# One transformer kernel, one core: the expert sum of the PEER layer, half as a dense pass and half as a gather

## The chip, the core and the metric

The kernel runs on one core of one Trainium2 chip, as one launch. The metric is the device time of that core in microseconds (us), the median of several runs. The core has five engines that run beside each other, each through its own list of instructions: TensorE (PE in the profile; PEld is its weight load), VectorE (DVE), ScalarE (ACT), GpSimd (POOL) and SyncE (SP). They wait for each other on semaphores. DMA transfers are started by SP (queue q1) and by POOL (queue q0, for transfers whose addresses are in a table in SBUF).

## What is computed

The reference runs two blocks on 256 tokens of width 2048, all in float32. The first block ends with a PEER layer (product-key experts); the second block begins with a norm of its result. Only the PEER layer and the norms behind it are touched. Cut to what matters:

```python
# per token: 8 heads, in each the 16 best of 128 x 128 experts (pairs of two key numbers)
# expert number = 128 * key0 + key1, 16384 experts; 8 * 16 = 128 picks per token
w    = softmax(scores of the 16 best)
dot  = sum(h * peer_down[expert])            # down row: 2048 floats, 8 KB
x    = x + gt2 * sum_picks(w * gelu(dot) * peer_up[expert])   # up row: 8 KB
x    = rmsnorm(x, final_g)                   # end of block 1
h    = rmsnorm(x, g_pre) ; proj = h @ w_in   # start of block 2
```

The 256 tokens are two blocks of 128 (`tb` 0 and 1), one token on each of the 128 partitions. "Pick" p (0 to 255) is the p-th pick of all 128 tokens of a block: picks 0 to 127 belong to block 0, 128 to 255 to block 1. One gather fetches one pick: 128 rows, one per partition.

## The kernel before

The program is five phases, with a barrier of all engines between them: modulation, projection and first block up to about 971 us, `phase_peer` (the touched one), then the second projection and the second merge. In the second part PE runs without a gap over weights that ACT and POOL split in two.

**phase_peer** starts with a short prelude: ACT and PE turn the keys and the normed tokens `h2`, PE makes the first queries and scores, DVE makes the lists of route 0. A "route" is one head of one block of tokens (16 routes); its lists give 16 picks. Then comes one loop over `G` = 0 to 127, two picks per G, written out on each engine:

- **POOL** (`block.gpsimd`, L1662 and L1670) issues per G two gathers of `peer_down` rows into `down_rows` and two of `peer_up` rows into `up_rows`, 1 MB each. Both tiles have 4 slots (`ROWS`), so a gather waits until the pick four before it has been used.
- **DVE** makes the two dot products of the G (L2057, 128x2048 each), then a part of the lists of a coming route at some G (`key_list` twice, `pair_list`, `pick_numbers`, `normalize`, at `lists_at(r)`: every 8 G up to route 7, then every 6 G, up to G = 104), then adds the up row of the even pick, times its share, to `expert_sum` (`add_even`, L2017, 128x2048).
- **ACT** makes gelu and share of the two picks and a diagonal matrix of the odd pick's share (`pick_diagonal`).
- **PE** adds the odd pick's up row by four matmuls of the diagonal with 512 columns each (L1764) into four PSUM banks. Between these it works through the remaining queries, the scores, and from `G = KV` on the key/value projection of `mem` for block 2 (L1792), whose weights SP loads through `weight_ring`.

At `G = TAIL` = 64 the sum of block 0 is complete; its residual, its norms and its turned copy are made inside the loop. After the loop the same is done for block 1 in four column pieces of 512, and the first weight tile of `w_in_2` is split.

An fp32 matmul stands in the trace as two records.

## Time and profile before

| | us |
|---|---|
| median of 3 runs (3496.9 to 3499.43) | 3499.34 |
| span of the profiled execution | 3498.0 |
| from its start to the first dot product of the loop | 1002.75 |
| end of the last dot product of the loop | about 2323.4 |
| first matmul of the second projection | 2349.80 |

The profiled execution is 1.3 us under the median of the runs. The page gives one line for each costly group of instructions, with its busy time, the mean of one, and the idle time just ahead of it on its engine with what ended that idle time. The timeline view gives start and length of single instructions. A duration can overlap the next one's start by some tens of ns, so where many of the same kind follow each other, the distance from start to start is the cost.

### The profile page before, as it was taken

The numbers are of one execution on the slowest core, as the hardware profiler recorded it, in microseconds if no ns is written. First come the engines' busy times: TensorE is split into PE (matmuls) and PEld (weight loads), VectorE is DVE, ScalarE is ACT, GpSimd is POOL, SyncE is SP. The second block draws the span as 40 slices with busy tenths as digits, with TensorE's granted clock in tenths as the row PEclk, the third lists the DMA queues.
The fourth block names the chain that finished last, engine by engine and source line by source line (L and its number), as shares of the span: only waits on it lengthen the run. The fifth ranks groups of instructions, "written<-read, shape, count | busy, mean of one in ns | idle before, by whom it ended". The sixth has DMA issues, their size and how long they took to land. (4 is left out here: it accounts for less than half of the span.)

```text
span 3498.0 us, 31036 instructions
## 1 busy us (share of the span) xinstructions
PE 2928.4 (84%) x11330; PEld 2066.9 (59%) x11330; DVE 1862.3 (53%) x2379; ACT 1143.5 (33%) x1853; POOL 2390.3 (68%) x1133
## 2 busy tenths in 40 slices
PE   5899999999976666665456776569999999999999
PEld 1687778788853333322122232238888888888887
DVE  0767365532457787868888787761137421111121
ACT  2422354454421111111122112124445344444443
POOL 0444675688836676757677666758767688888887
PEclk9999999999988888877777887779999999999999
DMA  9899753455669999999999999986545455666554
GB/s 414 296 346 347 248 165 127 133 193 187 234 263 427 425 427 425 427 425 428 415 427 427 425 427 404 427 336 202 172 155 191 133 181 193 212 204 204 191 188 169
DMA packets 305995, 1015.86 MB, mean 290 GB/s; under 512 B 21916, under 2 KB 26616, under 8 KB 234928
## 3 DMA queue, kind: packets, MB, share of 16 engines
q1 hardware_dynamic: 228870, 472.46, 39.1%
q0 software_dynamic: 73728, 536.90, 36.4%
q10 hardware_dynamic: 3244, 4.51, 0.3%
q8 instruction: 90, 1.47, 0.2%
q14 instruction: 63, 0.51, 0.0%
HBM read 1009.58 MB, written 4.23 MB: 290 GB/s over the span
## 5 line engine op out<-in xcount | busy, mean ns | idle before, releaser
L670 POOL TENSOR_TENSOR block_weights_lo<-weight_ring,block_weights_hi 128x1024 fp32r<-128x1024 f32 x608 | 1483.6, 2449 | 611.1 <-ACT block_weights_hi L663 498.6
L1764 PE MATMUL banks<-up_rows,pick_diagonal 128*128 128x512 f32 x1024 | 675.4, 821 | 469.4 <-DMA up_rows<-peer_up,picked_experts 403.1
L663 ACT ACTIVATE block_weights_hi<-weight_ring 128x1024 fp32r<-128x1024 f32 x608 | 641.2, 1059 | 976.0 <-PE banks L2831 315.8
L1764 PEld LDWEIGHTS banks<-up_rows,pick_diagonal 128*128 128x128 f32 x1024 | 261.8, 268 | 852.2 <-issue 745.6
L1670 POOL DMA_INDIRECT up_rows<-peer_up,picked_experts x256 | 477.4, 1865 | 338.2 <-PE banks L1764 113.4
L2057 DVE CUSTOM_DVE_ANT_0 down_rows<-down_rows,h_tokens 128x2048 f32<-128x2048 f32 x256 | 584.3, 2290 | 203.2 <-DMA down_rows<-peer_down,picked_experts 198.3
L1662 POOL DMA_INDIRECT down_rows<-peer_down,picked_experts x256 | 422.3, 1649 | 116.2 <-issue 79.5
L2017 DVE SCALAR_TENSOR_TENSOR expert_sum<-up_rows,pick_share,expert_sum 128x2048 f32<-128x2048 f32 x125 | 293.9, 2351 | 57.9 <-ACT pick_share L1887 52.7
L1881 ACT ACTIVATE pick_gelu<-pick_dots 128x2 f32<-128x2 f32 x127 | 25.8, 203 | 828.1 <-DVE pick_dots L2057 828.0
L2264 PE MATMUL banks<-block_weights_hi,h_T_hi 128*128 128x512 f32 x704 | 282.2, 401 | 2.7 <-PEq L1534 2.7
L2266 PE MATMUL banks<-block_weights_hi,h_T_lo 128*128 128x512 f32 x704 | 275.2, 391 | 0.0
L2265 PE MATMUL banks<-block_weights_lo,h_T_hi 128*128 128x512 f32 x704 | 274.8, 390 | 0.0
L2829 PE MATMUL banks<-block_weights_hi,h_T_hi 128*128 128x512 f32 x640 | 250.2, 391 | 0.0
L2831 PE MATMUL banks<-block_weights_hi,h_T_lo 128*128 128x512 f32 x640 | 249.3, 390 | 0.0
L2830 PE MATMUL banks<-block_weights_lo,h_T_hi 128*128 128x512 f32 x640 | 249.1, 389 | 0.0
L940 PE MATMUL banks<-block_weights_hi,h_T_hi 128*128 128x512 f32 x512 | 205.2, 401 | 6.8 <-POOL block_weights_lo L670 5.2
L589 DVE SCALAR_TENSOR_TENSOR banks<-cond_ring,cond_T,banks 128x512 f32<-128x512 f32 x224 | 169.3, 756 | 64.4 <-DMA cond_ring<-w_ada 57.6
L941 PE MATMUL banks<-block_weights_lo,h_T_hi 128*128 128x512 f32 x512 | 200.7, 392 | 0.0
L2895 DVE TENSOR_TENSOR gate<-banks,p_cols 128x512 f32<-128x512 f32 x32 | 20.6, 686 | 262.4 <-PE banks L2831 262.4
L2264 PEld LDWEIGHTS banks<-block_weights_hi,h_T_hi 128*128 128x128 f32 x704 | 132.6, 188 | 31.4 <-issue 4.8
L942 PE MATMUL banks<-block_weights_hi,h_T_lo 128*128 128x512 f32 x384 | 150.5, 392 | 0.0
L2266 PEld LDWEIGHTS banks<-block_weights_hi,h_T_lo 128*128 128x128 f32 x704 | 132.5, 188 | 28.3
(500 smaller groups left out, 4412.2 us busy)
## 6 DMA issues: line engine op xcount, KB each, us to landing
weight_ring<-w_in SPq DMA_DIRECT2D x232, 1024.0 KB, 5.0
cond_ring<-w_ada SPq DMA_DIRECT2D x128, 512.0 KB, 6.1
weight_ring<-w_ada SPq DMA_DIRECT2D x32, 1024.0 KB, 8.6
weight_ring<-w_out SPq DMA_DIRECT2D x32, 1024.0 KB, 5.0
weight_ring<-peer_query SPq DMA_DIRECT2D x16, 1024.0 KB, 16.3
weight_ring<-w_ret_out SPq DMA_DIRECT2D x8, 1024.0 KB, 4.9
weight_ring<-w_mlstm_out SPq DMA_DIRECT2D x8, 1024.0 KB, 4.9
weight_ring<-w_mem_kv SPq DMA_DIRECT2D x8, 1024.0 KB, 16.4
```

Of the source, the lines that this page charges most:

```text
L663: act.activation(self.hi[:, self.place(slot, h)], ring.tile[:, slot, h * self.HALF:(h + 1) * self.HALF], ACT.Copy).then_inc(self.hi_ready, 1)
L670: pool.tensor_tensor(self.lo[:, at], ring.tile[:, slot, h * self.HALF:(h + 1) * self.HALF], self.hi[:, at], ALU.subtract).then_inc(ring.us ...
L1662: pool.indirect_dma_start(down[:, p % ROWS], None, io["peer_down"][0], bass.IndirectOffsetOnAxis(ap=expert[:, p:p + 1], axis=0)).then_inc( ...
L1670: pool.indirect_dma_start(up[:, p % ROWS], None, io["peer_up"][0], bass.IndirectOffsetOnAxis(ap=expert[:, p:p + 1], axis=0)).then_inc(up_l ...
L1764: mm = pe.matmul(ps[:, 4 + b], diag[:, G % 2], up[:, p % ROWS, b * CG:(b + 1) * CG], start=(G % PER_TB == 0), stop=(G % PER_TB == PER_TB - ...
L2017: dve.scalar_tensor_tensor(acc[:], up[:, p % ROWS], share[:, p:p + 1], acc[:], ALU.mult, ALU.add).then_inc(even_added, 1)
L2057: dve.tensor_tensor_reduce(down[:, p % ROWS], down[:, p % ROWS], h2[:, G // PER_TB], 1.0, 0.0, ALU.mult, ALU.add, dots[:, p:p + 1]).then_i ...
L2264: pe.matmul(out, hi, w_hi, start=(k == 0), stop=False, skip_group_check=True)
L2265: pe.matmul(out, hi, w_lo, start=False, stop=False, skip_group_check=True)
L2266: mm = pe.matmul(out, lo, w_hi, start=False, stop=(k == KB - 1), skip_group_check=True)
L2829: pe.matmul(out, hi, w_hi, start=begin, stop=False, skip_group_check=True)
L2831: mm = pe.matmul(out, lo, w_hi, start=False, stop=end, skip_group_check=True)
```

## The change

All 256 down gathers come first, in a loop of their own; the up side follows. The 2048 columns of `peer_up` are cut in two halves:

- **Columns 0 to 1023 (dense)**: `peer_up[:, 0:1024]` is read whole, in 128 tiles of 128 experts (512 KB each, SP's queue, 4 slots `up_tiles`), and multiplied by a matrix of shares per expert and token (`share_of[tb]`, 128 x 128 x 128 floats), four matmuls per tile, into four PSUM banks. The matrix is made from the picks: for each token DVE makes two one-hot matrices over `iota` (`mark_tokens`: one of key1 times the share, one of key0), PE multiplies them (`spread_shares`), ACT copies the result for four tokens at a time (`keep_shares`). Block 0's matrix is made in the down loop at G = 88 to 119 (`A_AT` = 88), block 1's after it.
- **Columns 1024 to 2047 (wide)**: gathered as half rows (`expert_half`, 4 KB per row, 512 KB per gather) and all added by DVE in SBUF (`add_up`, 128x1024).

The share matrix of block 0 lies where `weight_ring`, `x_tokens` and `h_T` were, that of block 1 where the scores and `down_rows` were. So `x` is written to DRAM at the start of the phase and read back in the dense loop; three rows for the norms are read broadcast (3 MB), and the four tiles of `w_in_2` are loaded at tile 104. Norms of both blocks are made at the end, in 8 pieces of 512 columns (`PIECES`).

```diff
+        DENSE = D // 2
+        WIDE = D - DENSE
+        TOKENS = 4
+        A_GROUPS = P // TOKENS
...
+        PIECES = [(tb, N_DENSE + n) for tb in range(TB) for n in range(N_WIDE)] + [(tb, n) for tb in range(TB) for n in range(N_DENSE)]
...
         def _(sp):
+            sp.dma_start(iota[:], io["k_iota128"]).then_inc(iota_in, 16)
+            sp.dma_start(e.x_rows, e.x[:]).then_inc(x_spilled, 16)
...
+            sp.wait_ge(dot_done, TB * PICKS - ROWS)
+            for j in range(PEER_K):
+                if j >= ROWS:
+                    sp.wait_ge(blocks_done, j - ROWS + 1)
+                sp.dma_start(tile[:, j % ROWS], up_block(j)).then_inc(tile_landed[j % ROWS], 16)
+                if j == TOKENS_FREE + ROWS:
+                    sp.wait_ge(x_spilled, 16)
+                    sp.dma_start(x1[:], e.x_rows).then_inc(x_back, 16)
+                if j == ROWS_FREE + ROWS:
+                    for row, src in ((final_g, io["final_g"]), (gt2, e.mod_rows[0, 3 * D:4 * D]), (g_pre, io["g_pre_2"][0])):
+                        sp.dma_start(row, src.partition_broadcast(P)).then_inc(rows_in, 16)
+                if j == ROWS_FREE + 6 * ROWS:
+                    load_tiles(sp, ring, turn_of(io["w_in_2"][0], slice(SECOND_CHUNKS[0], SECOND_CHUNKS[0] + CG)), base + N + N_KV)
...
         def _(pool):
-            for G in range(GROUPS):
-                if G % PER_ROUTE == 0:
...
+            for p in range(TB * PICKS):
+                if p % R_PICKS == 0:
+                    pool.wait_ge(picks_ready, p // R_PICKS + 1)
+                if p >= ROWS:
+                    pool.wait_ge(dot_done, p - ROWS + 1)
...
+            pool.wait_ge(kv_out, N_KV * TB)
+            for p in range(TB * PICKS):
+                if p >= ROWS:
+                    pool.wait_ge(up_added, p - ROWS + 1)
...
+                pool.indirect_dma_start(up[:, p % ROWS], None, up_halves,
+                                        bass.IndirectOffsetOnAxis(ap=expert_half[:, p:p + 1], axis=0)).then_inc(up_landed[p % ROWS], 16)
...
+            def spread_shares(g):
+                pe.wait_ge(hots_ready, g + 1)
...
+                for j in range(TOKENS):
+                    mm = pe.matmul(ps[:, 6 + g % 2, j * P:(j + 1) * P], hot[:, g % 2, j, 0], hot[:, g % 2, j, 1], start=True, stop=True, skip_group_check=True)
...
+            def dense(j):
+                pe.wait_ge(tile_landed[j % ROWS], in_turn(j))
+                for tb in range(TB):
+                    for n in range(N_DENSE):
+                        mm = pe.matmul(ps[:, 2 * tb + n], share_of[tb][:, j], part(tile[:, j % ROWS], n), start=(j == 0), stop=(j == PEER_K - 1),
+                                       skip_group_check=True)
...
+            pe.wait_ge(a_out, TB * A_GROUPS)
+            pe.wait_ge(kv_out, N_KV * TB)
+            for j in range(PEER_K):
+                dense(j)
...
+            def mark_tokens(g):
...
+                for j in range(TOKENS):
+                    key = lambda i, t=t0 + j: cols[:, tb, i, t:t + 1]
+                    dve.tensor_scalar(hot[:, g % 2, j, 0], iota[:], key(1), key(2), ALU.is_equal, ALU.mult)
+                    x = dve.tensor_scalar(hot[:, g % 2, j, 1], iota[:], key(0), None, ALU.is_equal)
...
-                if G < GROUPS - 1:
-                    add_even(G)
...
+                if 0 <= G - A_AT < A_GROUPS:
+                    mark_tokens(G - A_AT)
+
+            EARLY_UPS = A_GROUPS // 2
+            for g in range(A_GROUPS, TB * A_GROUPS):
+                mark_tokens(g)
+                if g % 2:
+                    add_up(g // 2 - EARLY_UPS)
+            for p in range(EARLY_UPS, TB * PICKS):
+                add_up(p)
```

**On POOL.** The gathers of the loop before are a row of pairs; here are the first of them (`down_rows` and `up_rows` are the 4-slot tiles):

```order
L1662 DMA down_rows<-peer_down,picked_experts 128x2048 x2
L1670 DMA up_rows<-peer_up,picked_experts 128x2048 x2
L1662 DMA down_rows<-peer_down,picked_experts 128x2048 x2
L1670 DMA up_rows<-peer_up,picked_experts 128x2048 x2
L1662 DMA down_rows<-peer_down,picked_experts 128x2048 x2
```

Of the changed kernel, the whole of POOL's work in the phase:

```order
L1691 DMA down_rows<-peer_down,picked_experts 128x2048 x256
L1698 DMA up_rows<-peer_up,picked_expert_halves 128x1024 x256
L1704 TENSOR_TENSOR x_final<-x_again,tail_row_8095 128x512 x8
L671 TENSOR_TENSOR block_weights_lo<-weight_ring,block_weights_hi 128x1024
```

The two kinds no longer alternate, and an up gather is half as wide.

**On DVE, inside the loop.** Before, two dot products (each with the read of its accumulator) and one add of an up row make a G without lists:

```order
L2057 ISA down_rows,pick_dots<-down_rows,h_tokens 128x2048
L2057 ISA pick_dots 128x1
L2057 ISA down_rows,pick_dots<-down_rows,h_tokens 128x2048
L2057 ISA pick_dots 128x1
L2017 SCALAR_TENSOR_TENSOR expert_sum<-up_rows,pick_share,expert_sum 128x2048
```

After, around G = 88 (`pick_hot` holds the one-hot matrices), with a key list in the same G:

```order
L2084 ISA down_rows,pick_dots<-down_rows,h_tokens 128x2048
L2084 ISA pick_dots 128x1
L1524 MAX key_top<-key_scores 128x8
L1525 MAX_INDEX key_top_at<-key_top,key_scores 128x8
L1526 MATCH_REPLACE scores_left<-key_top,key_scores 128x128
L1527 MAX key_top<-scores_left 128x8
L1528 MAX_INDEX key_top_at<-key_top,scores_left 128x8
L2045 TENSOR_SCALAR pick_hot<-iota_8089,pick_cols 128x128
L2046 TENSOR_SCALAR pick_hot<-iota_8089,pick_cols 128x128
L2045 TENSOR_SCALAR pick_hot<-iota_8089,pick_cols 128x128
L2046 TENSOR_SCALAR pick_hot<-iota_8089,pick_cols 128x128
```

The add has left the loop, and from G = 88 to 119 eight mark instructions follow the dots and lists of each G.

**On DVE, behind the last dot product.** The changed kernel marks block 1's tokens there, eight instructions per group of four tokens, and puts one add of a half row (`wide_sums`) behind every second group:

```order
L2045 TENSOR_SCALAR pick_hot<-iota_8089,pick_cols 128x128
L2046 TENSOR_SCALAR pick_hot<-iota_8089,pick_cols 128x128
L2059 SCALAR_TENSOR_TENSOR wide_sums<-up_rows,pick_share,wide_sums 128x1024
L2045 TENSOR_SCALAR pick_hot<-iota_8089,pick_cols 128x128
L2046 TENSOR_SCALAR pick_hot<-iota_8089,pick_cols 128x128
```

In the kernel before nothing stands between the last dot product and the last pieces of the residual; here all of block 1's marks do, and PE's first dense matmul stands behind them.

## Rows read from the trace of the kernel before

**Rows 1.** A stretch: busy time (and count) by engine, granted clock, DMA share, GB/s

```profile
core 0: us, PE busy (x) PEld busy (x) DVE busy (x) ACT busy (x) POOL busy (x), PEclk, DMA share, GB/s
1005.00:2320.00 1315.00, 845.47 (x1729) 386.74 (x1728) 1038.19 (x1268) 222.33 (x628) 893.25 (x507) 0.80 1.01 424
```

**Rows 2.** Groups of instructions: busy, mean of one, idle before, releaser

```profile
L2057 DVE CUSTOM_DVE_ANT_0 down_rows<-down_rows,h_tokens 128x2048 f32<-128x2048 f32 x256 | 584.3, 2290 | 203.2 <-DMA down_rows<-peer_down,picked_experts 198.3
L2017 DVE SCALAR_TENSOR_TENSOR expert_sum<-up_rows,pick_share,expert_sum 128x2048 f32<-128x2048 f32 x125 | 293.9, 2351 | 57.9 <-ACT pick_share L1887 52.7 <-DVE key_top_at L1527 3.8 <-issue 0.5
L2046 DVE SCALAR_TENSOR_TENSOR h_tokens<-h_tokens,rstd,lat_cols 128x512 f32<-128x512 f32 x8 | 5.4, 747 | 0.0
```

**Rows 3.** Timeline of DVE through one route's lists: start us, us, instruction

```profile
1700.96 0.29 DVE L1523 MAX8 key_top<-key_scores 128x8 f32<-128x128 f32 x1
...
1703.00 2.35 DVE L2017 SCALAR_TENSOR_TENSOR expert_sum<-up_rows,pick_share,expert_sum 128x2048 f32<-128x2048 f32 x1 [0.24 <-DVE key_top_at L1527]
...
1707.48 2.29 DVE L2057 CUSTOM_DVE_ANT_0 down_rows<-down_rows,h_tokens 128x2048 f32<-128x2048 f32 x1
...
1709.70 0.42 DVE L1983 TENSOR_TENSOR pair_scores<-key_top 128x256 f32<-128x256 f32 x1
...
1712.77 2.35 DVE L2017 SCALAR_TENSOR_TENSOR expert_sum<-up_rows,pick_share,expert_sum 128x2048 f32<-128x2048 f32 x1
...
1719.46 0.17 DVE L1989 CAST key_top_number<-key_top_at 128x32 f32<-128x32 uint32 x1
...
1723.44 2.35 DVE L2017 SCALAR_TENSOR_TENSOR expert_sum<-up_rows,pick_share,expert_sum 128x2048 f32<-128x2048 f32 x1
...
1730.53 0.48 DVE L2005 TENSOR_SCALAR picked_weights<-picked_weights,softmax_sum 128x16 f32<-128x16 f32 x1
```

**Rows 4.** Timeline of POOL over the same time

```profile
1706.47 1.90 POOL L1670 DMA_INDIRECT up_rows<-peer_up,picked_experts  x1 [0.30 <-issue]
...
1710.88 0.94 POOL L1662 DMA_INDIRECT down_rows<-peer_down,picked_experts  x1 [0.30 <-issue]
...
1729.11 1.90 POOL L1670 DMA_INDIRECT up_rows<-peer_up,picked_experts  x1 [0.30 <-issue]
```

**Rows 5.** Single lines of DVE: durations in ns, minimum/median/maximum

```profile
L2005 DVE TENSOR_SCALAR picked_weights<-picked_weights,softmax_sum x16: 234/234/485, 997.0 to 2094.3; 128x16 f32<-128x16 f32 x16
L2572 DVE TENSOR_SCALAR p_cols<-p_cols,lse_weight x8: 273/275/2391, 2687.0 to 2740.3; 128x128 f32<-128x128 f32 x8
L566 DVE TENSOR_SCALAR x_tokens<-h_T,modulation_scale,modulation_cols x14: 397/401/2552, 98.8 to 133.4; 128x256 f32<-128x256 f32 x14
```

**Rows 6.** DMA packets from 1025 to 1060 us, by queue

```profile
q0 software_dynamic: 1597, 11.63, 78.7%
q1 hardware_dynamic: 1596, 3.17, 23.3%
```

**Rows 7.** Start of the loop: the first gather on POOL, the first dot

```profile
997.01 1.11 POOL L1662 DMA_INDIRECT down_rows<-peer_down,picked_experts  x1 [36.40 <-DVE picked_experts L1998]
...
1002.75 2.29 DVE L2057 CUSTOM_DVE_ANT_0 down_rows<-down_rows,h_tokens 128x2048 f32<-128x2048 f32 x1 [5.48 <-DMA down_rows<-peer_down,picked_experts]
```

**Rows 8.** Timeline of PE: four fp32 matmuls (8 records) of 512 columns

```profile
1994.30 3.67 PE L1764 MATMUL banks<-up_rows,pick_diagonal 128*128 128x512 f32 x8 [1.03 <-DMA up_rows<-peer_up,picked_experts]
1997.81 3.60 PE L1792 MATMUL banks<-weight_ring,h_T 128*128 128x512 f32 x8
...
2316.33 6.67 PE L1764 MATMUL banks<-up_rows,pick_diagonal 128*128 128x512 f32 x8 [3.35 <-DMA up_rows<-peer_up,picked_experts]
```

**Rows 9.** End of the phase: last dot and first pieces on DVE, PE's next phase

```profile
2321.18 2.29 DVE L2057 CUSTOM_DVE_ANT_0 down_rows<-down_rows,h_tokens 128x2048 f32<-128x2048 f32 x1 [0.21 <-DMA down_rows<-peer_down,picked_experts]
...
2328.36 0.70 DVE L2109 TENSOR_TENSOR banks<-banks,key_scores 128x512 f32<-128x512 f32 x1 [0.35 <-PE banks L1764]
...
2329.70 0.69 DVE L2109 TENSOR_TENSOR banks<-banks,key_scores 128x512 f32<-128x512 f32 x1
...
2349.80 0.76 PE L2264 MATMUL banks<-block_weights_hi,h_T_hi 128*128 128x512 f32 x1 [2.73 <-PEq L1534]
```

More of the change, by code:

```diff
@@ L2027, in inverse_roots @@
[L2027 to L2030 removed]
+                if p % PICKS == 0:
+                    if p:
+                        dve.wait_ge(a_out, TB * A_GROUPS)
+                    dve.tensor_scalar(acc, row, share[:, p:p + 1], None, ALU.mult).then_inc(up_added, 1)
+                else:
+                    dve.wait_ge(up_added, p)
+                    dve.scalar_tensor_tensor(acc, row, share[:, p:p + 1], acc, ALU.mult, ALU.add).then_inc(up_added, 1)
@@ L2111, in _ @@
[L2111 to L2124 removed]
+                if 0 <= G - A_AT < A_GROUPS:
+                    mark_tokens(G - A_AT)
@@ new lines, in _ @@
+            dve.wait_ge(x2_squared, len(PIECES))
+            step(dve.tensor_reduce(sums[:, 0], parts[:, 0], AX, ALU.add))
+            step(dve.tensor_scalar(var[:, 0], sums[:, 0], 1.0 / D, EPS, ALU.mult, ALU.add))
+            step(dve.reciprocal(inverse[:], var[:, 0]))
+            dve.wait_ge(xf_squared, len(PIECES))
+            step(dve.tensor_reduce(sums[:, 1], parts[:, 1], AX, ALU.add))
+            step(dve.scalar_tensor_tensor(var[:, 1], sums[:, 1], 1.0 / D, inverse[:], ALU.mult, ALU.mult))
@@ new lines, in _ @@
+            dve.tensor_scalar(var[:, 1], var[:, 1], EPS, None, ALU.add).then_inc(x2_var, 1)
+            dve.wait_ge(x2_root, 1)
+            step(dve.reciprocal(var[:], var[:]))
+            step(dve.tensor_tensor(pre_rstd[:], var[:, 0], var[:, 1], ALU.mult))
+            for fill in range(TB * FILLS_X + 1):
+                if fill < TB * FILLS_X:
+                    tb, f = divmod(fill, FILLS_X)
+                    dve.scalar_tensor_tensor(part(x1[:, tb], f), part(xf[:, tb], f), pre_rstd[:, tb:tb + 1], part(g_pre, f), ALU.mult, ALU.mult).then_inc(xn_ready, 1)
+                if fill:
+                    copy_lo(*divmod(fill - 1, FILLS_X))
```

392 lines of the change are left out of this document (162 added, 230 removed).

## The prediction

> **What bounds the kernel now.** I read the stretches first, then the groups, then single instructions. In the stretch of the gather loop the DMA engines are busy all the time, at 424 GB/s [rows 1]; the slots of that table to look at are the DMA share of 1.01 beside DVE's 1038 busy us of 1315. The groups say the same from the other side: DVE's dots sit idle 203 us in all, 198 of them for a down row [rows 2]. So the loop is a DMA stage, and its length is its bytes. What matters for the change is how far the next engine is behind: DVE is 79% busy over the loop, so it has only some 270 us to give.
>
> **The change in bytes.** Per pick 1.05 MB of down stay; up shrinks from 256 x 1.05 = 268 MB to 256 x 0.52 = 134 MB gathered and 128 x 0.52 = 67 MB read whole. That is 67 MB less, against some 9 MB more (x out and in 4, broadcast rows 3, rounded up for the first table). 58 MB at 424 GB/s are 137 us: the gain if DMA stayed the bound all through. I hold that it doesn't, because the change also cuts the phase in two: a down stage with all of DVE's dots and lists, then an up stage. DVE's work and the bytes were beside each other before; now the down stage has half the bytes and two thirds of DVE's work.
>
> **Down stage, by DVE.** DVE works its list in order.
> - Dots: start to start 2.22 us (1707.48 to 1709.70) [rows 3]; 256 x 2.215 = 567 us.
> - Lists of a route: a key list 1700.96 to 1703.00, 2.04 us, twice; the pair list 1709.70 to 1712.77, 3.07; the numbers 1719.46 to 1723.44, 3.98, and one small step more in the change, 0.2; normalize is three small steps, 0.6 [rows 3, 5]. Sum 11.9 us; 15 routes in the loop: 179 us. They had been beside a DMA-bound loop and cost nothing; now they are on the path.
> - Marks of block 0: 256 instructions of 128x128. No row has this form; the nearest are 275 ns (128 wide, one scalar per partition) and 401 ns (256 wide, two) [rows 5]. A dot lasts 2.29 and is followed after 2.21, so I take 0.08 off, and 0.07 for half the width: 0.20 and 0.26, 0.23 on average: 59 us. Bounds 0.16 (the 234 ns of a 16-wide one less 0.08) to 0.33: 41 to 84.
> - POOL against DVE. At 1706.47 POOL issues a gather, which takes 1.90 us, until 1708.37: 0.89 after the end of the dot that ran meanwhile (1707.48). Without a long DVE instruction a gather's issue takes 0.94 [rows 3, 4]. The other way round, the small TENSOR_SCALAR of 1730.53 lasts 0.48 instead of 0.234, and ends at 1731.01 with POOL's gather of 1729.11 [rows 3 to 5]. So a mark that meets a gather's issue waits for it, up to 0.9 us. 64 gathers are issued beside block 0's marks: 0 to 57 us; POOL is woken by dots that stand right ahead of the marks, so I take two thirds, 38.
> - DMA where no list stands: 37 of the 128 pairs have neither list nor mark. A pair is 2.1 MB, 4.95 us at 424 GB/s, against 4.43 of two dots: 19 us. Query weights in the same stretch share the queues: 5 us.
>
> Sum 567 + 179 + 59 + 38 + 19 + 5 = 867. The first dot stands at 1002.75 [rows 7]; nothing ahead of it changes but one 2 MB write. The last dot ends near **1870**. DMA alone would need 268 MB + 24 MB of weights, 690 us, so DVE is the bound by 177 us here.
>
> **Between the stages.** Dense matmuls wait for all of block 1's shares, and those for the last dot. Behind it: gelu, share, three transposes and a copy, 3 us; 256 marks, 59; 16 adds of half rows between them; 16 gathers issued against marks, 14. An add of 1024 columns lies between 747 ns at 512 and 2351 at 2048 [rows 2], 1.28, and with its own semaphore 1.33: 21 us. Sum 97: dense starts near **1967**. DMA has almost nothing to do here, since both kinds have four slots. This gap is new and nothing hides it.
>
> **Up stage, three streams beside each other.**
> - PE: 128 tiles of four fp32 matmuls. At the full clock four take 3.51 us (1994.30 to 1997.81) [rows 8]: 449 us. Tiles, x, broadcast rows and the four 1 MB weight tiles go through one SP queue; two queues with work get equal packets (1597 and 1596) [rows 6], so 9 MB ahead of a tile delay it by more than the 10 us that three tiles in flight cover: 20 us. 469.
> - DMA: 236 gathers and 124 tiles left, 189 MB, and 10 MB of others: 199 MB at 424 GB/s, 470 us.
> - Gathers and adds: 240 left. A slot's turn is add 1.33, issue 1.0 to 2.2, landing. The first gather's issue ends 998.12 and its dot starts 1002.75 [rows 7]: 4.6 us for 1.05 MB, of which 2.5 are transfer, so 2.2 fixed; half the bytes beside tiles add 1.2 to 2.5. Sum 5.7 to 8.2 us, by four slots 1.4 to 2.1; what tiles at 150 GB/s leave of 424 gives 1.9. I take 2.0: 480 us.
>
> All three lie within 11 us, which is how the halves were cut; the slowest with some unevenness, 485: the last add near **2452**.
>
> **Tail.** Before, from the first piece of the last block (2328.36) to the next phase's first matmul (2349.80) are 21.4 us [rows 9]. Now 8 pieces instead of 4 at 1.33 each (2328.36 to 2329.70) [rows 9], plus 5; four more turned pieces, plus 5; and the last add precedes it directly. 31 us: the next phase starts at 2483, where before it did at 2349.80. Behind that nothing changes: 3498.0 - 2349.8 = 1148.2.
>
> 1002.75 + 867 + 97 + 485 + 31 + 1148 = 3631 us of span; the median stands 1.3 above the profiled execution: **3632**. So 133 us slower: the down stage's DVE (177 over its bytes) and the gap (97) take more than the 137 of the bytes.
>
> **A rule against the trace.** POOL's issues wait for dots with two SBUF inputs [rows 3, 4]. The Trainium skill ("SBUF — State Buffer", Who interferes with whom) says that an instruction with two SBUF inputs contends with GpSimd only where GpSimd reads SBUF, and infers that writing descriptors doesn't. By that, adds would never hold back a gather, and the up stage would be DMA's 470: 3617. The trace differs: a gather's issue here takes 1.90 instead of 0.94. The same section says of tensor_scalar in its two-port mode that it and GpSimd shut each other out for a whole instruction, whoever comes first. That speaks against this change, which adds 512 of them; by it the full 57 us apply instead of 38, 3651. The TENSOR_SCALAR of 0.48 us agrees.
>
> **Rivals.**
> - *POOL's issues are the up stage's pace* (slower still). If each gather's issue is caught behind an add: 1.33 + 0.89 + 0.30 idle = 2.5 us, 240 x 2.5 = 600: 3747. For it: two of the three issues of [rows 4] were caught behind a DVE instruction. Against: a gather is woken by an add's end, and if DVE must then wait for data, POOL is free. 0.13.
> - *PE's clock stays at the low level in the dense pass.* In the loop, with PE busy 64%, the granted clock is 0.80 and four matmuls take up to 6.67 us [rows 1, 8]; at that 128 tiles are 854 us: 1967 + 854 + 31 + 1148 = 4000. Against: tiles get half of the queues' packets and need 150 GB/s, so PE should not pause, and the 3.51 are of a stretch with work at hand. If it falls only partly (4.5 a tile) it is 3720. 0.06.
> - *Marks and streams at their lower bounds*: marks 41 + 41, no hold by POOL, list-free pairs free, up stage 470: 3530. Still slower. 0.10.
> - *DMA stays the bound, faster*: the full 137 us and no gap are 3362; with the gap 3459. It decides at a DVE time under 690 us in the down stage; dots and lists alone are 746, from a dot of 2290 ns in the mean over 256 [rows 2]. 0.03.
> - *The change doesn't do what it says* (half rows moving whole rows, say): 67 to 134 MB more in the up stage, 3790 or more. 0.02.
>
> **How the numbers follow.** The forecast (3632, itself 3570 to 3700) has 0.66. The range leaves out the clock case, whole rows, and the outer parts of the others: 3545 to 3745. A measurement here can tell about 0.2%, 7 us. Faster by more: 0.03; within: 0.02; slower: 0.95.
>
> **What would show it.** Right: in the down stage DMA well under 424 GB/s (near 340) with DVE over 90% busy; last dot near 1870; some 95 us with DMA and PE nearly idle; then PE over 90% busy at clock 1.00, dense and adds ending within 30 us of each other. Wrong: dots waiting for down rows (then slots or DMA, not DVE, bound that stage), marks far from 0.23 us, a gather pace far from 2.0 us, PE pauses between tiles.

## The result, and the profile after

| | before | after |
|---|---|---|
| median, us | 3498.46 (3496.9 to 3499.43, 4 runs) | 3719.69 (3714.63 to 3720.43, 4 runs) |
| ratio | | 1.0631, interval 1.0616 to 1.0646 |
| profiled execution: span | 3498.0 | 3718.6 |

The change makes the kernel 221 us slower; 133 were forecast, in a range that holds the measured time. One run of the kernel with the split alone, 3825.43 us, fell in a slower state of the chip, and that kernel is compared without it. Where the 221 us come from is read in three tables.

The first is the table of stretches of the changed kernel, cut at the ends of its stages: the down stage, the gap, the up stage while the dense pass runs, and what is left of the gathers behind it. Columns as in [rows 1].

```profile
core 0: us, PE busy (x) PEld busy (x) DVE busy (x) ACT busy (x) POOL busy (x), PEclk, DMA share, GB/s
1003.00:1889.00 886.00, 274.63 (x945) 203.71 (x944) 786.96 (x1400) 173.02 (x523) 440.08 (x256) 0.61 0.87 331
1889.00:1970.00 81.00, 53.59 (x260) 47.22 (x261) 78.78 (x274) 20.27 (x36) 15.09 (x16) 0.69 0.35 106
1970.00:2440.00 470.00, 445.96 (x1024) 196.22 (x1024) 243.64 (x190) 1.24 (x2) 223.93 (x191) 0.97 0.98 370
2440.00:2537.00 97.00, 0.12 (x1) 0.00 (x0) 62.28 (x49) 0.00 (x0) 57.82 (x47) 0.52 0.79 259
```

In the down stage DVE is busy 787 of 886 us, and DMA moves 331 GB/s where the loop before moved 424 [rows 1]. In the gap DMA moves 106 GB/s and PE is busy 54 of 81 us. In the up stage PE is busy 446 of 470 us at a granted clock of 0.97, but the gathers don't keep up: only 190 adds fall into the 470 us, and 49 more take another 97 us with PE idle.

The second is the groups of the changed kernel (busy, mean ns of one, idle before, releaser), beside [rows 2]:

```profile
L2084 DVE CUSTOM_DVE_ANT_0 down_rows<-down_rows,h_tokens 128x2048 f32<-128x2048 f32 x256 | 579.6, 2288 | 80.1 <-DMA down_rows<-peer_down,picked_experts 76.3
L2059 DVE SCALAR_TENSOR_TENSOR wide_sums<-up_rows,pick_share,wide_sums 128x1024 f32<-128x1024 f32 x254 | 326.5, 1285 | 259.2 <-DMA up_rows<-peer_up,picked_expert_halves 255.1
L1773 PE MATMUL banks<-up_tiles,expert_shares 128*128 128x512 f32 x1024 | 446.3, 599 | 24.7 <-DMA up_tiles<-peer_up 24.0
L1698 POOL DMA_INDIRECT up_rows<-peer_up,picked_expert_halves x256 | 301.8, 1179 | 352.9 <-DVE wide_sums L2059 298.6
```

Adds wait 255 us for a row to land, and POOL waits 299 us for an add to free a slot. Neither engine is the bound of the up stage, and each waits for the other's slot. PE waited 24 us for tiles.

The third is the timeline of the changed kernel at the stage borders: the last dot; the first dense matmul; the last add; the first matmul of the next phase.

```profile
1886.37 2.29 DVE L2084 CUSTOM_DVE_ANT_0 down_rows<-down_rows,h_tokens 128x2048 f32<-128x2048 f32 x1 [1.46 <-DMA down_rows<-peer_down,picked_experts]
...
1969.79 6.71 PE L1773 MATMUL banks<-up_tiles,expert_shares 128*128 128x512 f32 x11 [0.69 <-ACT expert_shares L1899]
...
2536.40 1.28 DVE L2059 SCALAR_TENSOR_TENSOR wide_sums<-up_rows,pick_share,wide_sums 128x1024 f32<-128x1024 f32 x1 [0.23 <-DMA up_rows<-peer_up,picked_expert_halves]
...
2570.50 0.77 PE L2278 MATMUL banks<-block_weights_hi,h_T_hi 128*128 128x512 f32 x1 [2.78 <-PEq L1535]
```

| stage | forecast, us | measured, us | difference |
|---|---|---|---|
| down stage, to the last dot | 867 | 886.6 | +20 |
| gap, to the first dense matmul | 97 | 81.1 | -16 |
| up stage, to the last add | 485 | 567.9 | +83 |
| tail, to the next phase | 31 | 32.8 | +2 |
| the rest | 1148 | 1148.1 | 0 |

The differences sum to 89 us, and the measured median stands 88 over the forecast. Nearly all of it is the up stage, so most experiments are about what sets the gathers' pace there.

**The turn of a slot, read from the trace.** POOL and DVE of the changed kernel, in the middle of the up stage:

```profile
2157.46 0.94 POOL L1698 DMA_INDIRECT up_rows<-peer_up,picked_expert_halves  x1 [1.13 <-DVE wide_sums L2059]
2159.53 0.94 POOL L1698 DMA_INDIRECT up_rows<-peer_up,picked_expert_halves  x1 [1.13 <-DVE wide_sums L2059]
```

```profile
2155.36 1.30 DVE L2059 SCALAR_TENSOR_TENSOR wide_sums<-up_rows,pick_share,wide_sums 128x1024 f32<-128x1024 f32 x1 [1.08 <-DMA up_rows<-peer_up,picked_expert_halves]
2157.44 1.28 DVE L2059 SCALAR_TENSOR_TENSOR wide_sums<-up_rows,pick_share,wide_sums 128x1024 f32<-128x1024 f32 x1 [0.79 <-DMA up_rows<-peer_up,picked_expert_halves]
```

The add of 2155.36 ends at 2156.66, and the issue that it frees starts at 2157.46: 0.80 later (the next pair: 2158.72 and 2159.53, 0.81). From the start of a gather's issue to its landing the same stretch (1975 to 2430 us) has a median of 7.5:

```profile
DMA to landing us min/median/max: 5.2/7.5/11.6
```

The landing includes the issue's 0.94 (a lone issue; the very first lasts 1.11). The first gather of the changed kernel starts its issue at 996.43 and lands after 5.6, at 1002.03, where the first dot starts. So a slot's turn is landing 7.5 + add 1.28 + waking POOL 0.8 = 9.6, and with four slots 2.40 us a gather. Measured: 470 us for 190 adds, 2.47.

The rest of the turn shows when the 183 gathers issued in that stretch are paired one by one. Landings are 7.65 in the mean; a landed row waits 0.09 for its add (0.54 at most, so rows don't queue for DVE); and from an add's end to the issue that it frees are 0.81 in the median, but 0.95 in the mean, since 64 of the 183 issues stand 0.3 behind another issue of POOL and come 1.12 or more after the add. 7.65 + 0.09 + 1.28 + 0.95 are 9.97, by four 2.49.

```profile
  DVE wide_sums L2059: 214.7, 118
  issue: 24.8, 64
```

That a quarter of the turn is the pace holds for any four slots in a ring, whatever sets the landing. It doesn't show yet that the slots are the cause: with full DMA engines the landing would just be longer. The experiments have to show that.

### The profile page after: what moved, and what is told of

It reads as the page before. It is cut to its first block and busy times, and to the rows that moved or that the text cites. A ratio compares the mean times of both kernels' runs of the same rounds, so it can differ in the third digit from the quotient of the medians.

```text
span 3718.6 us, 32668 instructions
## 1 busy us (share of the span) xinstructions
PE 2850.0 (77%) x11816; PEld 2124.4 (57%) x11816; DVE 2000.2 (54%) x3035; ACT 1120.3 (30%) x1796; POOL 2237.6 (60%) x1137
## 5 line engine op out<-in xcount | busy, mean ns | idle before, releaser
L1691 POOL DMA_INDIRECT down_rows<-peer_down,picked_experts x256 | 439.0, 1715 | 477.9 <-DVE pick_dots L2084 375.7
L2084 DVE CUSTOM_DVE_ANT_0 down_rows<-down_rows,h_tokens 128x2048 f32<-128x2048 f32 x256 | 579.6, 2288 | 80.1 <-DMA down_rows<-peer_down,picked_experts 76.3
L1698 POOL DMA_INDIRECT up_rows<-peer_up,picked_expert_halves x256 | 301.8, 1179 | 352.9 <-DVE wide_sums L2059 298.6
L2059 DVE SCALAR_TENSOR_TENSOR wide_sums<-up_rows,pick_share,wide_sums 128x1024 f32<-128x1024 f32 x254 | 326.5, 1285 | 259.2 <-DMA up_rows<-peer_up,picked_expert_halves 255.1
L1773 PE MATMUL banks<-up_tiles,expert_shares 128*128 128x512 f32 x1024 | 446.3, 599 | 24.7 <-DMA up_tiles<-peer_up 24.0
L1773 PEld LDWEIGHTS banks<-up_tiles,expert_shares 128*128 128x128 f32 x1024 | 196.4, 192 | 274.1 <-issue 246.6
L1766 PE MATMUL banks<-pick_hot 128*128 128x128 f32 x512 | 118.9, 409 | 263.3 <-DVE pick_hot L2046 263.3
L2280 PE MATMUL banks<-block_weights_hi,h_T_lo 128*128 128x512 f32 x704 | 275.3, 391 | 0.0
L1766 PEld LDWEIGHTS banks<-pick_hot 128*128 128x128 f32 x512 | 103.5, 300 | 278.7 <-DVE pick_hot L2046 278.6
L2845 PE MATMUL banks<-block_weights_hi,h_T_lo 128*128 128x512 f32 x640 | 249.3, 390 | 0.0
L1721 PE MATMUL banks<-h_T,weight_ring 128*128 128x256 f32 (+1 forms) x576 | 145.4, 421 | 27.8 <-DMA weight_ring<-peer_query 26.4
```

Of the source, the lines that this page charges most:

```text
L1691: pool.indirect_dma_start(down[:, p % ROWS], None, io["peer_down"][0], bass.IndirectOffsetOnAxis(ap=expert[:, p:p + 1], axis=0)).then_inc( ...
L1698: pool.indirect_dma_start(up[:, p % ROWS], None, up_halves, bass.IndirectOffsetOnAxis(ap=expert_half[:, p:p + 1], axis=0)).then_inc(up_lan ...
L1773: mm = pe.matmul(ps[:, 2 * tb + n], share_of[tb][:, j], part(tile[:, j % ROWS], n), start=(j == 0), stop=(j == PEER_K - 1), skip_group_che ...
L2059: dve.scalar_tensor_tensor(acc, row, share[:, p:p + 1], acc, ALU.mult, ALU.add).then_inc(up_added, 1)
L2084: dve.tensor_tensor_reduce(down[:, p % ROWS], down[:, p % ROWS], h2[:, G // PER_TB], 1.0, 0.0, ALU.mult, ALU.add, dots[:, p:p + 1]).then_i ...
L2280: mm = pe.matmul(out, lo, w_hi, start=False, stop=(k == KB - 1), skip_group_check=True)
```

## Experiments

Two questions. For the up stage: **B**, the pace is four slots by the turn of one; against **A**, the DMA engines are full (share 0.98) and give 370 GB/s because of what the transfers are, so that less time in the turn only makes the landing longer. For the down stage: DVE's list is the bound, or the slots, or the bytes. Each kernel was run beside the kernel before (medians 3497.77, 3499.65 or 3497.87 us); the ratios are to it.

### The split alone

Two stages as in the change, but no dense pass and no marks: whole up rows are gathered, and DVE adds all 256 of them. In the kernel before, PE added half of them.

```diff
-        DENSE = D // 2
+        DENSE = 0
...
-                pool.indirect_dma_start(up[:, p % ROWS], None, up_halves,
+                pool.indirect_dma_start(up[:, p % ROWS], None, io["peer_up"][0],
...
-            for j in range(PEER_K):
-                dense(j)
```

> The changed kernel with the split into two stages kept, but without the dense pass: all 256 down gathers first, then 256 gathers of whole up rows (8 KB), all added by VectorE in SBUF (128x2048 each); no marks, no share matrix, no tiles. Nothing is left out of the result. Theory S (the split itself costs, since VectorE's dots and lists leave the cover of the bytes, and the dense pass gains nothing beside it): the down stage is VectorE's 567 + 179 + some 75 of waits, so the last dot ends near 1825 instead of 1889; the up stage is 256 x 2.47 us = 633 at 424 GB/s; with the tail 33 and the rest 1148 the time is 3660 to 3680, some 50 us faster than the changed kernel and 165 slower than before. Rival D (the dense half earns its bytes): at 67 MB less than this one the changed kernel would be the faster of the two by up to 67 MB / 424 GB/s = 158 us, so this one would take 3800 or more. If an issue of GpSimd is caught behind every long add, the pace is 2.9 us and the time 3775.

Measured: 3782.79 (3768.6 to 3799.04, three runs; with the fourth, 3825.43, the median is 3790.92), ratio 1.0870 (1.0814 to 1.0925); by the two medians of 3782.79 and 3497.77 it is 1.0815. The split as built here costs 285 us, and the change is 63 us faster than it. Of what had been expected, only the last case came: issues caught behind every long add, 3775. The 285 aren't the price of two stages alone: DVE has also taken over the 128 adds that PE did before. A split in which PE keeps them was not run. In the up stage of this kernel POOL's issues of 0.94 have become 2.3:

```profile
L1691 POOL DMA_INDIRECT up_rows<-peer_up,picked_experts x256: 932/2315/3041, 1844.1 to 2571.3; - x128
```

```profile
2097.89 2.17 POOL L1691 DMA_INDIRECT up_rows<-peer_up,picked_experts  x1 [0.31 <-issue]
2100.37 2.70 POOL L1691 DMA_INDIRECT up_rows<-peer_up,picked_experts  x1 [0.30 <-issue]
2103.38 2.38 POOL L1691 DMA_INDIRECT up_rows<-peer_up,picked_experts  x1 [0.30 <-issue]
```

```profile
2099.91 2.35 DVE L2031 SCALAR_TENSOR_TENSOR wide_sums<-up_rows,pick_share,wide_sums 128x2048 f32<-128x2048 f32 x1 [0.66 <-DMA up_rows<-peer_up,picked_experts]
2102.59 4.84 DVE L2031 SCALAR_TENSOR_TENSOR wide_sums<-up_rows,pick_share,wide_sums 128x2048 f32<-128x2048 f32 x2 [0.33 <-DMA up_rows<-peer_up,picked_experts]
```

The issue of 2100.37 ends at 2103.07, 0.81 after the add that it ran beside (2102.26). That is the rival "POOL's issues are the pace" of the prediction, which the split brings out with adds of 2048 columns (2.78 us a gather: 300 us for 108 issues). In the changed kernel the median issue is 0.94, because the add is short.

### The split alone, adds of half a row

The kernel above with adds of 1024 of the 2048 columns (the other columns' sum is left out; the gathers still fetch whole rows).

```diff
+                if p % PICKS:
+                    acc, row = acc[:, 0:D // 2], row[:, 0:D // 2]
```

> The split-alone kernel (no dense pass, whole up rows of 8 KB gathered), with the adds over the first 1024 columns only (the rest is left out). There the pace was 2.83 us per gather, each issue took 2.2 to 2.7 us because it was caught behind an add of 2.35 us. By the turn: 7.4 landing + 2.3 issue + 2.35 add with a share of overlap = 11.4 in four slots. With adds of 1.28 the issue falls to some 1.1 and the add by 1.07: 9.4 / 4 = 2.35, below the engines' 2.5 for 1.05 MB at 420 GB/s, so the pace is 2.5 and the time 3785 - 256 x 0.33 = 3700. If the engines' rate at this pattern were the limit (387 GB/s at 2.83 us), the time stays near 3790.

Measured: 3691.65 (3683.89 to 3705.09), ratio 1.0555 (1.0526 to 1.0584), 91 us under the kernel above (73 between the ends of the up stages of the two profiled executions), near the 3700 expected. The bytes are the same, the issue's median is back at 936 ns, and DMA is full, at the rate of [rows 1]:

```profile
L1691 POOL DMA_INDIRECT up_rows<-peer_up,picked_experts x256: 932/936/2516, 1844.2 to 2498.8; - x128
```

```profile
2200.00:2480.00 280.00, 0.00 (x0) 0.00 (x0) 145.58 (x114) 0.00 (x0) 106.56 (x114) 0.50 1.01 424
```

So with long adds it was DVE and its hold on POOL that kept the up stage under the DMA rate. How much of it is the hold (1.4 us less per issue) and how much the shorter add in the turn (1.07 less) these two runs don't separate.

This kernel is also 28 us faster than the changed one, though it fetches 67 MB more. It isn't complete, but its adds are as long as those of the change. So the 63 us by which the change beats the split alone are no proof that the dense pass pays: at equal adds the whole rows, without marks, gap and tiles, came out ahead.

### Dots of half a row

The dot products over 1024 columns instead of 2048 (the other half of each product is left out); all bytes as in the change.

```diff
-                    dve.tensor_tensor_reduce(down[:, p % ROWS], down[:, p % ROWS], h2[:, G // PER_TB], 1.0
+                    dve.tensor_tensor_reduce(down[:, p % ROWS, 0:D // 2], down[:, p % ROWS, 0:D // 2], h2[:, G // PER_TB, 0:D // 2], 1.0
```

> The changed kernel, with each dot product over the first 1024 columns only (the other half of it is left out); the gathers of down rows are unchanged. If VectorE's list sets the down stage: a dot goes from 2.21 us to some 1.15, VectorE's sum falls by 270 and the stage meets the bytes (292 MB at 424 GB/s, 690 us) and the slots: 886 becomes 700 to 740, so the whole is 150 to 185 us faster, near 3550. If the bytes or the four slots set it, the time stays within 30 us of 3720.

Measured: 3594.63 (3593.09 to 3601.2), ratio 1.0274 (1.0257 to 1.0292): 125 us less than the change, short of the expected 150 to 185. Table of stretches and group:

```profile
1003.00:1760.00 757.00, 280.55 (x941) 203.60 (x939) 520.39 (x1399) 172.80 (x521) 274.19 (x256) 0.62 0.97 386
```

```profile
L2084 DVE CUSTOM_DVE_ANT_0 down_rows<-down_rows,h_tokens 128x1024 f32<-128x1024 f32 x256 | 310.9, 1223 | 209.3 <-DMA down_rows<-peer_down,picked_experts 208.0
```

DVE lost 267 us of work, the stage 129: DVE's list was the bound, by that much and no more. Behind it don't come the bytes at 424 GB/s (690 us) but 757 us, with DVE waiting 208 us for rows at 386 GB/s.

### Six slots for the down rows

Two more slots for down rows, in memory that is free then.

```diff
+        DOWNS = 6
+        more = place("down_more", [P, DOWNS - ROWS, D], S0 + ROWS * WIDE * 4)
+        down_row = lambda p: down[:, p % DOWNS] if p % DOWNS < ROWS else more[:, p % DOWNS - ROWS]
...
-                if p >= ROWS:
-                    pool.wait_ge(dot_done, p - ROWS + 1)
+                if p >= DOWNS:
+                    pool.wait_ge(dot_done, p - DOWNS + 1)
```

> The changed kernel with six slots for down rows instead of four; nothing else. VectorE waited 76 us for down rows in the changed kernel, mine said 24. If the turn of a slot (dot, issue held by the next dot, fixed latency, transfer) is the reason, six slots cut that wait to 20 to 30 us and the whole by 45 to 55, near 3670. If it is the shared queue (query weights in 2 KB packets), only the waits of the last 18 picks go: 10 to 15 us.

Measured: 3678.66 (3670.37 to 3680.39), ratio 1.0508 (1.0491 to 1.0526), 41 us less, a little under the 45 to 55 expected; the last dot ends at 1842.7, 46 earlier. Its waits for rows fell from 76.3 to 27.0 us:

```profile
L2087 DVE CUSTOM_DVE_ANT_0 down_rows<-down_rows,h_tokens 128x2048 f32<-128x2048 f32 x172 | 387.3, 2286 | 24.1 <-DMA down_rows<-peer_down,picked_experts 21.4
L2087 DVE CUSTOM_DVE_ANT_0 down_more<-down_more,h_tokens 128x2048 f32<-128x2048 f32 x84 | 189.6, 2286 | 6.7 <-DMA down_more<-peer_down,picked_experts 5.6
```

Where DVE has only dots in its list, the down stage too is paced by four slots.

### Marks only once

Only the first two groups of four tokens are marked, one for each buffer; the other groups' marks are left out, everything else is issued as before.

```diff
             def mark_tokens(g):
+                if g >= 2:
+                    return
```

> The changed kernel, with the one-hot matrices written only for the first two groups of four tokens; TensorE and ScalarE use these two for all 64 groups, so the shares are wrong, but as much is multiplied, copied and transferred. Prices the marks: 248 of 256 leave the down loop (0.23 us each, 57 us, and up to 38 for holds by GpSimd's issues, of which the trace shows few), and between the stages 256 leave (59 us). The gap of 81 us shrinks to what TensorE's share products need at the low clock, 32 x 1.2 to 1.4 = 40 to 45. Together 90 to 105 us faster, near 3620. If holds had cost the 38 of the forecast, 130.

Measured: 3646.1 (3637.97 to 3655.35), ratio 1.0418 (1.0392 to 1.0443), 74 less than the change, under the expected 90 to 105. The gap shrinks by 45 us (1858.1 to 1894.1 instead of 1888.7 to 1969.8), but the down stage only by 31, though 58 us of marks are gone from it. Its waits for rows rise from 76 to 97 us, since marks had stood where DVE would else have waited.

```profile
L2088 DVE CUSTOM_DVE_ANT_0 down_rows<-down_rows,h_tokens 128x2048 f32<-128x2048 f32 x256 | 581.2, 2290 | 101.2 <-DMA down_rows<-peer_down,picked_experts 96.5
```

### The up stage without adds, without tiles, without both

Three kernels take the terms of the turn away one by one. In the first the adds are left out and a gather waits only until the row four before it has landed; in the second only 4 of 128 tiles are read and multiplied; the third does both. The second and third were timed once; in them the reads of `x`, of the broadcast rows and of `w_in_2` come right behind the four tiles.

```diff
-                    pool.wait_ge(up_added, p - ROWS + 1)
+                    pool.wait_ge(up_landed[p % ROWS], in_turn(p - ROWS))
...
-            for j in range(PEER_K):
+            for j in range(ROWS):
                 dense(j)
```

> The changed kernel without the 256 adds of half rows (left out; two short instructions write the sums instead): a gather waits only until the one four before it has landed. Theory A (the DMA engines are full: 4 KB rows go at 371 GB/s, not 424): the pace of gathers beside tiles stays set by the engines, DMA stays between 365 and 380 GB/s while both run, and the time falls only by the 21 us of adds in the gap, the gathers that now run in the gap (some 23 MB, 60 us) and the end without tiles: 3630 to 3650. Theory B (the turn of a slot sets the pace, with the add in it): the turn loses 1.3 us, the pace goes from 2.37 to 1.9 or less, DMA reaches 420 GB/s, and TensorE's 470 us set the stage: 3590 to 3605.

> The changed kernel with only 4 of the 128 tiles (the rest of the dense pass left out), adds kept. Shows the turn of a slot by itself: 2.0 us per gather, as at the end of the changed kernel when no tile was left, so the last add near 1968 + 240 x 2.02 = 2453 and the time near 3635. Theory A: then 2.37 beside tiles is the engines, and 2.0 the turn. Theory B: 2.3 or more here too.

> As the run without adds, and with only 4 of the 128 tiles of the dense pass (124 loads and 496 matmuls left out): 4 KB rows by GpSimd's queue alone. GpSimd's issue allows one gather per 1.24 us, 423 GB/s. Theory A: the engines are full below that, 1.40 us or more per gather, 375 GB/s or less at a DMA share of 1.0. If 4 KB rows cost nothing by themselves and only two queues beside each other do: 1.24 to 1.28 us, 410 to 423 GB/s.

Measured: without adds 3596.18 (3593.51 to 3599.16), ratio 1.0277 (1.0260 to 1.0294); without tiles 3643.61; without both 3504.6. The stretches of the three, in this order:

```profile
2000.00:2400.00 400.00, 371.65 (x849) 163.48 (x848) 0.00 (x0) 0.00 (x0) 176.07 (x188) 0.96 1.02 409
```

```profile
2000.00:2400.00 400.00, 0.00 (x0) 0.00 (x0) 252.78 (x198) 0.00 (x0) 246.49 (x196) 0.50 0.81 268
```

```profile
2000.00:2300.00 300.00, 0.00 (x0) 0.00 (x0) 0.00 (x0) 0.00 (x0) 170.40 (x182) 0.50 0.91 324
```

Without adds the same 4 KB rows and the same tiles move at 409 GB/s: the 370 of the change is no limit of the transfers, and A falls. (That 409 GB/s at a share of 1.02 stay 15 under the 424 of whole rows is left open.) The time is the one that B gave, the pace isn't: 2.13 us a gather, where B had 1.9 or less. Medians of the landing over the whole run, and the turn by it:

| tiles / adds | landing | + add | + wake | turn / 4 | measured pace (us / gathers) |
|---|---|---|---|---|---|
| yes / yes | 7.5 | 1.28 | 0.8 | 2.40 | 470 / 190 = 2.47 |
| yes / no | 7.3 | 0 | 0.9 | 2.05 | 400 / 188 = 2.13 |
| no / yes | 5.6 | 1.28 | 0.8 | 1.92 | 400 / 196 = 2.04 |
| no / no | 5.7 | 0 | 0.9 | 1.65 | 300 / 182 = 1.65 |

(Wake is the 0.8 read above; where a landing wakes POOL it is 0.9: single pairs of the second and last kernel give 0.87 and 0.89 in the mean. The first row's landing is that of its stretch.) The sums come within 0.12 us of the pace, as they must, since they are its parts. What the rows show is that the landing hardly answers to the adds (7.5 against 7.3, 5.6 against 5.7), so an add's time taken out of the turn is gained, while the tiles lengthen it by 1.6 to 1.9 us. The last run was a miss for what I had expected of it on either theory: at 324 GB/s DMA isn't full there, and POOL still waits for rows to land. A transfer of 512 KB that meets no tile and no add takes 5.7 us to land, so even four of them in flight don't fill the DMA engines.

### Tiles as rows of 8 KB

64 tiles of whole rows (1 MB, 8 KB in a row) with two slots, instead of 128 of half rows with four. Bytes and matmuls are the same; the sum is wrong, since the rows of half the experts are not read.

```diff
-up, tile = place("up_rows", [P, ROWS, WIDE], S0), place("up_tiles", [P, ROWS, DENSE], S0 + ROWS * WIDE * 4)
+up, tile = place("up_rows", [P, ROWS, WIDE], S0), place("up_tiles", [P, ROWS // 2, D], S0 + ROWS * WIDE * 4)
```

> The changed kernel, with the dense tiles read as 64 tiles of 8 KB rows (whole rows of 128 experts, two slots of 1 MB) in place of 128 tiles of 4 KB rows: same bytes, same number of matmuls, half the packets on that queue; the columns multiplied are the wrong ones for half of them. Theory A: 4 KB packets take 0.167 us of an engine, 8 KB ones 0.30; 16384 of the former are 171 us of the stage's 570, 8192 of the latter 154: 15 to 20 us faster, DMA near 383 GB/s beside 371. If the packet's size doesn't matter: no change, or up to 20 us slower by TensorE's pauses with two slots.

Measured: 3720.12 (3715.77 to 3729.46), ratio 1.0626 (1.0609 to 1.0644), no difference from the change. PE waited 61 us for tiles instead of 24 and the rate stayed at 366 GB/s. Longer rows give nothing, though coarser slots may have hidden a small gain.

### Five slots for half rows, three for tiles

The same memory, cut in another way.

```diff
+        UPS, TILES = 5, 3
-                if p >= ROWS:
-                    pool.wait_ge(up_added, p - ROWS + 1)
+                if p >= UPS:
+                    pool.wait_ge(up_added, p - UPS + 1)
```

> The changed kernel with five slots for gathered half rows and three for dense tiles, instead of four and four; same SBUF. Theory B, now in numbers: a slot's turn is landing + issue + add and its waits, 7.0 + 0.94 + 1.28 + 0.3 = 9.5 us beside tiles, and the pace is a quarter of it (2.37 measured); a fifth of it is 1.9. The last add comes 240 x (2.37 - 1.95) = 100 us earlier at most; by then the dense pass (469 us, three slots of 3.5 us against a landing of 6.7 leave it some pauses) is as late: the stage is 480 to 500 instead of 568, the time 3635 to 3655. DMA reaches 410 GB/s. If the engines were full at 371 GB/s, a fifth slot changes nothing: 3710 to 3725, with landing times up by a quarter (8.8 us).

Measured: 3648.0 (3645.65 to 3652.85), ratio 1.0432 (1.0415 to 1.0450): 72 us less, as B expected, where full engines gave 3710 to 3725. The turn did grow, from 9.98 to 10.62 us (mean of single gathers): of the 0.50 us a gather that a fifth slot gives at an unchanged turn, 0.37 came (2.49 to 2.12), not the 1.9 expected. With five slots the engines are near full as well. The rate is 401 GB/s with the same bytes in the same memory, and gathers and tiles now end together near 2462, PE waiting 48 us for tiles:

```profile
2000.00:2400.00 400.00, 353.23 (x797) 150.55 (x795) 242.67 (x189) 0.00 (x0) 248.39 (x189) 0.94 1.01 401
```

```profile
L1774 PE MATMUL banks<-up_tiles,expert_shares 128*128 128x512 f32 x1024 | 453.5, 602 | 49.6 <-DMA up_tiles<-peer_up 48.4
```

### Six down slots and five up slots

Both changes of slots in one kernel.

> The changed kernel with both: six slots for down rows, and five for half rows with three for tiles. The two cuts lie in different stages, so they add: 41 us of the one and 70 to 85 of the other, 3595 to 3610. Still slower than before by about 100: VectorE's sum in the down stage (567 + 179 + 59) and the gap stay.

Measured: 3605.73 (3601.72 to 3614.05), ratio 1.0313 (1.0296 to 1.0330). The two add up: 114 us less, of 41 and 72. The last dot ends at 1844.0, the last add at 2420.2. It is the best complete version of the changed form, and still 108 us slower than the kernel before, which the experiments don't reach: even the one that leaves out all adds and nearly all tiles takes 3504.6.

## Why the prediction was right, and where it was not

**Direction and form: right.** DVE as the bound of the down stage, a gap in front of the dense pass, a dense pass at a granted clock of 0.97, and a rest of 1148 came as worked out. The half-length dots show the first (267 us off DVE's work, 129 off the stage). The gap was less empty than forecast: 106 GB/s, and PE busy 54 of 81 us.

**The number: in the range, in part by luck.** 3719.69 lies outside the 3570 to 3700 given to the forecast's own mechanism. It is inside 3545 to 3745 only because the range also took in parts of rivals that didn't occur. Two of the prediction's own signs came out against it: dots waited 76 us for down rows, and the dense pass and the adds ended 98 us apart (2440.1 and 2537.7), not within 30. What the sum had wrong is a size, not a path: one term, the gathers' turn in the up stage.

**Down stage (867, measured 886.6): near by two misses that nearly cancel, which is luck.** Dots 567, marks 58 and waits for rows 76 are 701 of the 886.6; the 186 left are the lists and small waits, the lists taken at 179.
- Dots and marks were sized well (256 dots take 567 us from start to start, as forecast). Marks were taken at 0.23 us; eight in the timeline of the changed kernel take 1707.43 - 1705.61 = 1.82, 0.228 each:

```profile
1705.61 0.35 DVE L2045 TENSOR_SCALAR pick_hot<-iota,pick_cols 128x128 f32<-128x128 f32 x1
...
1707.43 2.28 DVE L2084 CUSTOM_DVE_ANT_0 down_rows<-down_rows,h_tokens 128x2048 f32<-128x2048 f32 x1
```

- Holds by POOL, 38 us: this term failed. The 256 marks with two scalars have 335 ns in the median and 518 at most, over both the down stage and the gap:

```profile
L2045 DVE TENSOR_SCALAR pick_hot<-iota,pick_cols x256: 327/335/518, 1607.7 to 1966.4; 128x128 f32<-128x128 f32 x128
```

  The other 256 marks reach 491. No mark lasted more than 0.22 us over its median, and from start to start marks beside an issue come hardly later (0.26 us from 1959.73 to 1959.99, as elsewhere). The term is a few us at most. The issues weren't held by marks either: the 15 in the gap, with marks all around, last 936 to 939 ns (1896.1 to 1964.1), where the forecast had put 14 us.

- Waits for rows, 19 + 5: this term failed too, and more: 76.3 us. I had taken list-free pairs as bound by the bytes (4.95 us a pair against 4.43). It is the slots. The last 18 picks, with neither list nor mark, are the clearest: from 1829.9 to 1886.4 in 17 steps, 3.3 us each, not 2.48. Their gathers land 9.6 us after the start of their issue, 2.0 of which are the issue itself, caught behind dots; 9.6 + 2.29 + 0.8 = 12.7, by four slots 3.2.

```profile
DMA to landing us min/median/max: 8.0/9.6/12.3
```

  Six slots took 49 of the 76 us away.

**Gap (97, measured 81): right in kind.** DVE is busy 78.8 us there: 256 marks at 0.228 are 58, and the adds among them 20. With the 3 us ahead of the first mark nothing is left for the 14 of holds. Without marks the gap is 36, of which PE is busy 34, nearly all with the 128 small matmuls of block 1's shares (256 records).

**Up stage (485, measured 568): the term that was mis-sized.** PE's 469 was 470, and its 20 us of waiting were 24. DMA's 470 at 424 GB/s would have held only at a rate that the slots didn't allow. The failed step is "I take 2.0" for the gathers. The turn was summed as 5.7 to 8.2 us, 8.0 by what I took; it is 9.98. In the prediction's own terms:

| term of the turn | taken, us | measured beside tiles (mean) |
|---|---|---|
| add | 1.33 | 1.28 |
| issue | 1.0 to 2.2 | 1.17 |
| issue's end to landing | 3.4 to 4.7 | 6.48 |
| landing to the add, and an add's end to the issue it frees | nothing | 1.04 |

The last term was put at nothing without a reason. The third was built on the very first gather [rows 7], 4.6 us for twice the bytes, less half of their transfer; but without tiles and adds the half-size transfer takes 4.8 behind its issue (5.7 with it), so halving the bytes took nothing off, and tiles add another 1.9 to 2.1. The landings in the middle of the loop had not been looked at. The 2.0 us is what the gathers take with no tiles beside them: 1.98 in the last 97 us here, 2.04 in the kernel without tiles. In the 470 us beside tiles 190 gathers at 2.47 instead of 2.0 are 89 us; the 49 behind them ran at 1.98, as taken. 89 less the 5 us of unevenness that I had added is the difference of 83.

**Rivals.** POOL's issues as the pace (2.5 us, 3747) came close in its number, 2.47 beside tiles, but not in its reason: the median issue is 0.94, POOL stands idle 215 of some 455 us for an add, and the adds wait for data. It is what happens with adds of 2048 columns. The clock stayed at 0.97 in the dense pass. DMA as the bound and lower-bound cases didn't occur.

**The rule against the trace.** The time doesn't decide between what I set against the Trainium skill's rules; single instructions do.

```profile
L1698 POOL DMA_INDIRECT up_rows<-peer_up,picked_expert_halves x194: 932/936/947, 1975.7 to 2388.4; - x194
L1698 POOL DMA_INDIRECT up_rows<-peer_up,picked_expert_halves x183: 932/938/1981, 1976.0 to 2429.3; - x183
```

Without adds (first line) all 194 issues last 932 to 947 ns; in the changed kernel (second line) they reach 1981, and beside adds of 2048 columns the median is 2315. So an add with two SBUF inputs does hold back a gather's issue, and the step "by that, adds would never hold back a gather" failed. But it failed as a reading of the rule: the Trainium skill ("SBUF — State Buffer", Who interferes with whom) says that an instruction with two SBUF inputs contends with a GpSimd instruction that reads SBUF, and a gather reads its row numbers there (`picked_expert_halves` in the lines above). By that part of the rule the trace agrees. Whether the writing of descriptors is held as well, which the same section infers it isn't, no run here separates.

Its other rule, that tensor_scalar in the two-port mode and GpSimd shut each other out for a whole instruction, would have made marks last up to 0.9 us longer; of the 256 marks of L2045 none lasted more than 518 ns, and the 15 issues beside marks took their usual 0.94 us. No run here shows whether those marks ran in that mode.

## What to carry to other kernels

Where a stage streams through a few slots, work out its pace as the slot's whole turn over the number of slots (issue to landing as seen beside the transfers of that stage, plus the use, plus the wake-up), and take the landing from the middle of a busy stretch, never from the first transfer. The landing itself depends on what else is in flight, so measure it again after a change. A loop that is bound by DMA hides its lists and dots for nothing; cutting it in two stages to save bytes can lay them bare, so sum the other engines' work stage by stage first. And when one kind of slot has an engine waiting and the other kind hasn't, moving one slot across costs no memory: it was worth 72 us here.

## What the runs showed of the hardware that I had not expected

- **The DMA share doesn't tell that the rate is reached.** At a share of 0.98 the changed kernel's up stage moved 370 GB/s; with the same kinds of transfers and a share of 1.02 it moved 409 (no adds), and the gathers of whole rows alone 424 at 1.01. In the down stage without long dots, 0.97 stood for 386. A share just under 1 hid some 10% here.
- **More slots for the gathers raised the rate at equal memory**: 370 to 401 GB/s, with one slot taken from the tiles.
- **Landing under load** (from the start of the issue, medians): 512 KB gathers landed in 5.6 to 5.7 us by themselves and in 7.3 to 7.5 beside 512 KB tiles; 1 MB gathers in 7.4 to 8.5, and in 9.6 near the end of the down stage (1830 to 1880 us). Tiles aren't the reason there: the first is issued at 1873.01, and the split alone, which has none, lands in 9.1 to 9.9 from 1792 to 1823 us. The reason stays open.
- **From an add's end to the start of the issue that it frees are 0.81 us** in the median of 183 pairs, 1.12 where another issue stands just ahead, and a freed slot pays it every turn.
- **An add of 1024 columns and two SBUF inputs stretched issues of GpSimd from 0.94 to as much as 1.98 us; marks with one SBUF tensor input didn't** (15 issues of 0.94 among them).
